# A two-block transformer kernel: gate convolution said two blocks later, quadrant forms begun one inner tile earlier, one more quadrant pair in the second MLP

## The reference

```python
h = rmsnorm(x, ln_ffn_g)
a, u = jnp.split(h @ w_ffn_in, 2, axis=-1)     # 1024 -> 2 x 2816
a = causal_dwconv(a, conv_w, conv_b)           # three taps along the tokens
x = x + (jax.nn.silu(a) * u) @ w_ffn_out       # 2816 -> 1024
```

## Time and profile before

| | |
|---|---|
| median of three runs | 1432.08 us |
| the profiled execution, its own time | 1431.07 us |
| its span in the trace | 1429.3 us |
| PE busy | 1415.7 us, 99% |
| DVE busy | 986.3 us, 69% |
| ACT busy | 647.3 us, 45% |
| granted PE clock, mean | 0.997 |

### The profile page before, as it was taken

How to read it: one execution, slowest core, us unless ns; L and a number is a source line. 1 busy time by engine, 2 the same in 40 slices (tenths; PEclk the granted TensorE clock), 3 DMA queues, 4 the chain that set the end, 5 groups by cost and what they waited for, 6 DMA issues and landing times.

```text
span 1429.3 us, 20561 instructions
## 1 busy us (share of the span) xinstructions
PE 1415.7 (99%) x8054; PEld 1215.2 (85%) x8054; DVE 986.3 (69%) x1537; ACT 647.3 (45%) x1028; POOL 214.3 (15%) x136
## 2 busy tenths in 40 slices
PE   9999999999999999999999999999999999999998
PEld 6776898889989888887789888888888879999997
DVE  5777477876676657897696726544553788888877
ACT  5345545534345424545465546323242545455550
POOL 4175324000000012330052104000021000000000
PEclk9999999999999999999999999999999999999999
DMA  6222112333223332222211111323232233323331
GB/s 241 89 75 74 60 60 89 98 98 116 94 99 104 124 98 74 89 74 75 74 61 45 60 45 60 117 89 103 90 99 93 74 99 108 104 91 117 104 106 72
DMA packets 36352, 130.00 MB, mean 91 GB/s; under 512 B 4040, under 2 KB 4296, under 8 KB 36256
## 3 DMA queue, kind: packets, MB, share of 16 engines
q1 hardware_dynamic: 35968, 128.44, 27.8%
q10 hardware_dynamic: 288, 0.26, 0.1%
HBM read 126.56 MB, written 2.10 MB: 90 GB/s over the span
## 4 chain that ended last, share of the span: by engine, by line
PE 91%; DVE 5%; ACT 3%; DMA 1%; issue 1%; ACTq 0%; DVEq 0%; SPq 0%
PE P L1720 17%; PE P L1722 16%; PE P L1721 16%; PE P L1701 6%; PE P L1703 6%; PE P L1702 6%; PE P L1768 4%; PE P L1759 4%; PE P L1761 4%; PE P L2061 2%; PE P L1808 1%; PE P L1809 1%; PE P L1810 1%; DVE WL L2554 1%; ACT WH L2148 1%
## 5 line engine op out<-in xcount | busy, mean ns | idle before, releaser
L2148 ACT ACTIVATE WH<-WR 128x1024 fp32r<-128x1024 f32 x212 | 223.5, 1054 | 260.1 <-PE P L1722 181.7
L2554 DVE TENSOR_TENSOR WL<-WR,WH 128x1024 fp32r<-128x1024 f32 x196 | 265.4, 1355 | 103.1 <-ACT WH L2148 102.6
L1720 PE MATMUL P<-AH,WH 128*128 128x512 f32 x456 | 186.3, 409 | 0.4 <-DVE WL L2554 0.3
L1722 PE MATMUL P<-AH,WL 128*128 128x512 f32 x456 | 178.2, 391 | 0.0
L1721 PE MATMUL P<-AL,WH 128*128 128x512 f32 x456 | 177.8, 390 | 0.0
L1720 PE MATMUL P<-FH,WH 128*128 128x512 f32 x432 | 168.6, 390 | 2.5 <-issue 2.3
L1721 PE MATMUL P<-FL,WH 128*128 128x512 f32 x432 | 168.4, 390 | 0.0
L1722 PE MATMUL P<-FH,WL 128*128 128x512 f32 x432 | 168.1, 389 | 0.0
L3369 POOL TENSOR_TENSOR AC<-AC,SQ 128x512 f32<-128x512 f32 x27 | 42.5, 1574 | 506.6 <-ACT SQ L2203 505.8
L1701 PE MATMUL P<-AH,WH 128*128 128x256 f32 x400 | 113.4, 284 | 0.4 <-ACT SN L2159 0.4
L1703 PE MATMUL P<-AH,WL 128*128 128x256 f32 x400 | 113.2, 283 | 0.0
(11 more groups left out here) (409 smaller groups left out, 3151.3 us busy)
## 6 DMA issues: line engine op xcount, KB each, us to landing
WR<-in_ws SPq DMA_DIRECT2D x212, 512.0 KB, 3.5
WX<-in_ws SPq DMA_DIRECT2D x21, 512.0 KB, 3.5
out<-Y SPq DMA_DIRECT2D x8, 256.0 KB, 2.0
H<-in_xT SPq DMA_DIRECT2D x3, 512.0 KB, 7.6
C<-in_const SPq DMA_DIRECT2D x1, 946.5 KB, 10.8
H<-in_xT SPq DMA_DIRECT2D x2, 256.0 KB, 4.2
PR<-in_pT SPq DMA_DIRECT2D x1, 512.0 KB, 4.4
WR<-in_ws SPq DMA_DIRECT2D x1, 384.0 KB, 4.5
```

The lines of the kernel that those rows point to most:

```text
L1720: e.matmul(P, wh, xh, start=start, stop=False)
L1722: ins = e.matmul(P, wl, xh, start=False, stop=stop)
L2148: e.activation(H, w_source(m, order, k), ACT.Copy).then_inc(*at.up("w_hi", "w_hi", k))
L2554: e.tensor_tensor(L, w_source(m, order, k), H, ALU.subtract).then_inc(*at.up("w_lo", "w_lo", k))
```

## The change

Three things are changed. The gate's convolution is taken out of `ffn_a`: the step `ffn_a` now scales on DVE and does the last tap on ACT, and a step `conv` says the two other taps and the SiLU. In the head, `conv` 0 and 1 come after both `ffn_a` 0 and 1; in plain tiles `conv` is said two blocks after `ffn_a`. The forms begin at inner tile 4. Plain tiles are 4 to 6, one chunk of the down projection follows them (with form 4's split two blocks into it), and pairs run from tile 7 on, fifteen of them.

```diff
+        def conv(f):
+            self.say("ffn_taps", f)
+            self.say("ffn_silu", f)
+        first(0, out[0])
+        self.paced(lambda: first(1, out[1]), lambda: conv(0), lambda: conv(1),
+                   lambda: second(0, out[2]), lambda: second(1, out[3]), lambda: first(2, out[4]),
+                   lambda: first(3, out[6]), lambda: conv(2), lambda: second(2, out[5]))
+        t = self.tile(fu(3), A)
+        conv(3)
+        second(3, t)
 
         def plain(f):
             first(f, self.tile(fa(f), A))
+            self.paced(lambda: None, lambda: None, lambda: conv(f))
             t = self.tile(fu(f), A)
             second(f, t)
...
-        for f in range(4, 8):
-            if f == 5:
+        for f in range(4, 7):
+            if f == 4:
                 self.beside(self.forms("5", 4))
             plain(f)
         self.align()
         d0, d1, d2 = (down(n) for n in range(3))
-        chunks(d0, 1)
-        self.say("t_split", "5", 4)
+        self.paced(lambda: None, lambda: None, lambda: self.say("t_split", "5", 4))
         chunks(d0, 1)
         self.finish()
         self.banks = (0, 1, 2, 3, 6, 7)
-        for f in range(8, 22):
+        for f in range(7, 22):
             pair(f)
             chunks(d0 if f < 10 else d1 if f < 16 else d2, 1)
...
     def ffn_a(f, t):
         ffn_tap(f)
-        ffn_silu(f)
...
         at.also(("ffn_a", f), "read", t.id)
-        ffn_taps(f)
```

## The result

The changed kernel takes 1436.54 us (median of 6, 1435.18 to 1437.52), the kernel before beside it 1432.20 (median of 6): 1.0030 times as long, 95% interval 1.0018 to 1.0042. So it is 4.3 us slower. The forecast was 1436.4. The profiled execution took 1437.44 us, with a span of 1435.6. In both profiles the copy of the norm's factors (RBC), which opens the gate's work on DVE, starts at 1108.81, so the times of the two can be set side by side as they stand.

What follows compares the result with a forecast made beforehand. DVE's queue, with ACT and one transfer, bounds the ramp to the first pair: its last product comes 11.34 us earlier, one more 15.54 us pair with chunk follows. Taken as +4.3 on 1432.08: 1436.4 us, range 1431.5 to 1440.0.

Steps and rivals of the forecast that it cites:

- The exchange: Last plain tile becomes a fifteenth pair: PE work falls 0.81 us, but DVE's queue adds waits; net +4.3 us.
- The taps' two waits of 0.9 us: In plain tiles, DVE's taps wait 0.88 us for ACT behind the scaling; forecast to stay.
- Rival C: Clock falls to half behind PE's 3.7 us wait ahead of the chunk, costing up to 1.6 us: 1438, chance 0.14.
- the 0.3 and 1.7 us waits: PE waits on DVE's queue: 0.3 us after the chunk, 1.7 us before the first pair's third product.
- The 1.6 that was kept for the range: Possible cost in us of half clock behind PE's long wait; counted as nothing in the sum.
- Rival B: In tiles 4 to 6 a low weight part fills the taps' 0.9 us waits: 2.7 us earlier, 1433.7, chance 0.22.
- E: Later taps save no DVE wait, `ffn_u` 3 stays at 1127.65, chain 3 us later still: 1439.4, chance 0.07.
- D: All PE waits up to the first pair's end vanish, 4.8 us faster: 1427.3, chance 0.07.
- from the second pair on queues and distances are those of now: Behind the first pair nothing changes: each pair with its chunk takes 15.54 us, no further loss.

Runs made afterwards that it cites:

- the late sums: Changed kernel with the first pair's three sums said behind the low part of the down projection's chunk: 1.0038 times the kernel before.
- the busy PE: Changed kernel with fourteen matmuls on old data filling PE's long wait ahead of the chunk: 1.0039 times the kernel before.
- the POOL run: Changed kernel with five plain low weight parts, in and before the chunk, on POOL instead of DVE: 1.0068 times the kernel before.
- the repeat: The changed kernel measured again, nothing altered: 1.0033 times the kernel before, 325.5 us from the RBC copy to the end.
- the taps undone: Changed kernel with taps and SiLU again right behind the scaling, forms at tile 4 and fifteen pairs kept: 1.0058 times the kernel before.
- the taps a block later: Changed kernel with the two other taps said one block later still in the plain tiles: 1.0020 times the kernel before.
- the two last kernels: Changed kernel's taps moved one block later, but fourteen pairs as before the change: forms at tile 4, 0.9976, or at tile 5, 0.9971 times the kernel before.

## Why the prediction was right

Its walk through DVE's queue, step by step:

| step | forecast | measured |
|---|---|---|
| `ffn_u` 3 | 1124.6 | 1124.71 |
| form 2 | 1127.67 | 1127.77 |
| low part in tile 5 | 1141.36 | 1141.46 |
| low part behind it | 1147.79 | 1147.89 |
| low part of the chunk | 1152.92 | 1153.02 |
| PE's wait ahead of the chunk | 3.7 | 3.62 |
| form 4's low part | 1163.0 | 1163.10 |
| half low part | 1164.73 | 1164.84 |
| sums of the next pair | 1168.88 | 1169.10 |
| last product of the first pair | 1171.79 | 1172.00 |

**The exchange.** Without waits PE would be 16.35 us sooner at the first pair; DVE's queue is only 9.4 sooner at form 2 and 11.1 at the sums ahead of the pair's last product, and the balance is paid in waits: 9.2 us measured where 9.1 were forecast. That the loss is the length of DVE's queue up to that product, and not where PE's waits stand or the clock behind them, was tried by the late sums and the busy PE (no change in either) and by the POOL run, where that queue got 4.4 us longer and the product came 4.45 us later. The taps' two waits of 0.9 us, taken out, gave back 2.0. A queue with less work in it was not reached: POOL cost DVE more than it took over.

**Rival C's mechanism happened at no price.** The clock did fall, and I had taken nothing for it since DVE's waits behind would absorb it. They did: the 0.3 and 1.7 us waits became 0 and 0.46, and with the clock held at 1.00 they were 0.36 and 1.62. The 1.6 that was kept for the range was not needed here.

**Rival B** was excluded rightly, by a detail told wrongly: for the low part to come first the taps need not stand behind the fifth block but one block later. Its price of 2.7 us was 2.0, since in the last tile SiLU is late next. **E** was excluded by `ffn_u` 3, and its 3 us are the delay's worth, as its undoing showed within the uncertainty. **D** is out by 9 us.

**What failed** is the sentence that from the second pair on queues and distances are those of now, and with it the chain's return to PE by 1172. The chain's start off PE, too, was forecast near 1139 and lies at 1109.5, right behind the RBC copy: DVE and ACT have the whole ramp on the chain, not its last 33 us. Later pairs still wait 0.1 to 0.3 us ahead of their last product, with a restart of 0.1: 2.4 us in sum from 1185 on, where before has 0.3. So the profiled execution is 6.3 us behind, 4.4 at the first pair and 1.9 later; it was forecast at 1435.4 and took 1437.44. In the repeat these waits sum to 1.0, and its stretch from RBC to the end is 5.0 longer than before's. They are in every profile with fifteen pairs (1.0 to 2.4 us) and all but gone with fourteen (0 to 0.6), so the step is wrong and not only unlucky. The forecast had +4.3 us and the medians show +4.3: that they agree to the tenth, while the two profiles show 5.0 and 6.3, is luck. From transfer to transfer the round of half low part, transfer and sums takes 15.2 to 16.8 us in the chain above, 15.7 on average, against 15.54 for a pair with its chunk on PE, so a delay is hardly made up; transfers in it vary from 3.35 to 4.39 us. What makes the sum differ between executions was not tried and stays open.

## What to carry to other kernels

When a stage is bound by a second engine's queue, removing work from PE only moves PE's arrival; carry each step of that queue through in the new order, and compare the two advances. Look for steps of a full queue that wait for a third engine, and say other work between: moving the taps by one block more was worth 1.5 thousandths here, 2 us, where a pair in place of a plain tile saves PE 0.81. Before work is moved to POOL, see what DVE does meanwhile.

## What the hardware showed that was not expected

POOL's parts of 2.4 to 3.1 us held up DVE steps by up to 2.2 us each. Behind idles of PE of 3.3 to 3.5 us the granted clock was at 0.50 to 0.52 for 3 to 6 us (the changed kernel and its repeat, the taps undone, the taps a block later), and behind one of 6.64 us at 0.52 for 4.7 (POOL); behind 2.24 us, in the run with late sums, it stayed at 1.00. And the fall of the earlier trace rows in the first block is not in every execution: from 189 to 193 us the clock is 0.57 in the profiles of the kernel before and the changed one, but 1.00 in those of the late sums and of the two last kernels, whose RBC comes some 1.8 us sooner (1106.97 to 1107.02). Distances from RBC were compared for that reason.
